# A two-model forward pass in one kernel: the prologue's token transfers, splits, banks and first two blocks rearranged

## What is computed

```python
meta = jnp.broadcast_to(meta_tokens.astype(x.dtype)[None], (b, N_META, D_MODEL))
h = jnp.concatenate([meta, x], axis=1)
...
hn = rms_norm(h, g_mix[layer])          # mean of squares, rsqrt, gain
z = h @ w_in                            # in attention_mixer, h is hn there
c_q, c_kv, k_pe, fq, fk, fv, f_logit = jnp.split(z, _offsets(ATTN_SPLITS), axis=-1)
...
bias = rel_table[t5_causal_bucket(jnp.maximum(dist, 0))]   # second model
```

## Time and profile before

| | |
|---|---|
| median of 3 runs | 1233.04 us |
| lowest, highest | 1232.21 us, 1683.81 us |
| profiled execution, its time | 1232.03 us |
| profiled execution, its span | 1230.2 us |
| PE busy | 1206.8 us, 98% of the span |
| DVE, ACT, POOL busy | 902.2, 713.7, 247.4 us |
| HBM traffic | 170 GB/s mean |

### The profile page before, as it was taken

The page is one execution under the profiler, slowest core; times in us unless marked ns, Lnnn a source line. Parts: engine busy times, 40 slices in busy tenths (PEclk is TensorE's granted clock), DMA queues, the critical chain, the costliest instruction groups (busy, mean ns, idle before and its releaser), DMA issues.

```text
span 1230.2 us, 23640 instructions
## 1 busy us (share of the span) xinstructions
PE 1206.8 (98%) x8096; PEld 1101.8 (90%) x8096; DVE 902.2 (73%) x1562; ACT 713.7 (58%) x1303; POOL 247.4 (20%) x260
## 2 busy tenths in 40 slices
PE   7999999999999999999999999999999999999997
PEld 5998899999999988888889988888889999888886
DVE  5788876555556988776568869776667988877764
ACT  4657756564444556664446876665444797666343
POOL 3000014220000114440011003442001811444000
PEclk9999999999999999999999999999999999999999
DMA  7514326555657565655556426665655644656550
GB/s 225 160 35 134 104 72 204 185 190 167 193 188 223 177 191 181 198 177 185 192 179 197 145 96 206 178 198 176 201 163 175 211 138 142 218 181 194 177 200 35
DMA packets 194922, 208.79 MB, mean 170 GB/s; under 512 B 6159, under 2 KB 183565, under 8 KB 194717
## 3 DMA queue, kind: packets, MB, share of 16 engines
q1 hardware_dynamic: 191861, 202.73, 51.7%
q10 hardware_dynamic: 2984, 5.06, 1.3%
HBM read 206.69 MB, written 2.64 MB: 170 GB/s over the span
## 4 chain that ended last, share of the span: by engine, by line
PE 86%; DVE 8%; ACT 3%; issue 2%; DMA 1%; POOL 0%; ACTq 0%; DVEq 0%; SPq 0%; POOLq 0%
PE PS L1922 27%; PE PS L1923 14%; PE PS L1916 10%; PE PS L1917 10%; PE PS L1918 9%; PE PS L2499 2%; PE PS L2500 2%; PE PS L2501 2%; DVE wlo L1075 2%; ACT whi L535 1%; PE PS L2101 1%; PE PS L2167 1%; PE PS L2145 1%; DVE x L1052 1%; PE PS L2263 1%
## 5 line engine op out<-in xcount | busy, mean ns | idle before, releaser
L535 ACT ACTIVATE whi<-raw 128x1024 fp32r<-128x1024 f32 x370 | 388.7, 1053 | 318.1 <-PE PS L1923 172.5
L1075 DVE TENSOR_TENSOR wlo<-raw,whi 128x1024 fp32r<-128x1024 f32 x370 | 454.2, 1234 | 161.4 <-ACT whi L535 158.2
L1922 PE MATMUL PS<-x,whi 128*128 128x512 f32 x832 | 291.7, 395 | 1.0 <-DVE x L1052 1.0
L1916 PE MATMUL PS<-x,whi 128*128 128x258 f32 (+2 forms) x800 | 231.9, 290 | 2.6 <-DVE wlo L1075 2.0
L1923 PE MATMUL PS<-x,wlo 128*128 128x256 f32 x832 | 234.4, 282 | 0.0
L1917 PE MATMUL PS<-x,whi 128*128 128x258 f32 (+2 forms) x800 | 228.7, 286 | 0.0
L1918 PE MATMUL PS<-x,wlo 128*128 128x258 f32 (+2 forms) x800 | 227.0, 284 | 0.0
L1922 PEld LDWEIGHTS PS<-x,whi 128*128 128x128 f32 x832 | 156.3, 188 | 37.2 <-DVE x L1052 1.6
L1825 POOL TENSOR_TENSOR act_s<-act_r 128x256 f32<-128x256 f32 (+1 forms) x128 | 142.9, 1116 | 213.4 <-ACT act_r L597 151.6
L1922 PE MATMUL PS<-hid,whi 128*128 128x512 f32 x512 | 179.0, 396 | 0.2
L1805 POOL TENSOR_TENSOR acc<-acc,sq 128x256 f32<-128x256 f32 (+2 forms) x64 | 51.8, 809 | 594.7 <-ACT sq L579 253.6
(11 more groups left out here) (323 smaller groups left out, 2009.6 us busy)
## 6 DMA issues: line engine op xcount, KB each, us to landing
raw<-in_mlp_w SPq DMA_DIRECT2D x64, 1024.0 KB, 5.3
raw<-in_w_mlp_up SPq DMA_DIRECT2D x32, 1024.0 KB, 5.5
raw<-in_w_mlp_down SPq DMA_DIRECT2D x32, 1024.0 KB, 5.0
raw<-in_w_in_conv SPq DMA_DIRECT2D x12, 1024.0 KB, 5.1
raw<-in_attn_w_in SPq DMA_DIRECT2D x12, 1024.0 KB, 5.1
raw<-in_mlstm_w_in SPq DMA_DIRECT2D x12, 1024.0 KB, 5.5
raw<-in_w_in_attn SPq DMA_DIRECT2D x9, 1024.0 KB, 5.9
raw<-in_w_out_attn SPq DMA_DIRECT2D x4, 1024.0 KB, 5.3
```

What stands on the lines that cost most here:

```text
L535: A(part_view(whi, b), raw_view(b), ACT.Copy).then_inc(w_hi, 1)
L1075: V.tensor_tensor(part_view(wlo, b), raw_view(b), f32(part_view(whi, b)), ALU.subtract).then_inc(w_lo, 1)
L1916: mm(dst, whi_b, xs_hi, start=first, stop=False)
L1922: mm(dst.rearrange("p (a t) -> p a t", a=2), std_cols(whi[b % RING], k), xs_both, start=first, stop=False)
```

## The change

Token transfer: `x_tok` comes in two transfers, features 0 to 511 (semaphore `x_in`) and 512 to 1023 (`x_right`). Meta tokens and both vector tables are issued by ACT, between the identity and the one-hot table. PE first runs 24 matmuls (`WARM`) of 256 columns on a buffer of ones (the still unused `wlo[3]`) into bank 7; their result is not read. The one-hot product moves from ahead of the token transposes to behind block 2. Transposed pieces go to eight different banks (`x_bank`), `xh` and `xl` are made straight from PSUM, and `h` is copied later; the squares read `h`. Blocks 0 and 1 are computed in halves: pieces 0 to 3 of both, then 4 to 7 of both. Blocks 4 and 5 go to banks 6 and 7, and their weights are split before the norm. The norm's matmul moves behind block 3. DVE and POOL no longer wait for `rel_out`; the bias rows lie in `act_r`, so two squares later in the layer wait for it on ACT.

```diff
-            sp.dma_start(x_tok[:, :, :], d["x"][0].rearrange("(a p) n -> p a n", p=P)).then_inc(Z["x_in"], 16)
-            sp.dma_start(meta_tok[:, :], d["meta_tokens"]).then_inc(Z["x_in"], 16)
-            sp.dma_start(vrow_a[:, :], d["v_rows_a"]).then_inc(Z["vec_in"], 16)
-            sp.dma_start(vrow_b[:, :], d["v_rows_b"]).then_inc(Z["vec_in"], 16)
+            sp.dma_start(x_tok[:, :, 0:HALF], x_rows[:, :, 0:HALF]).then_inc(Z["x_in"], 16)
+            sp.dma_start(x_tok[:, :, HALF:D], x_rows[:, :, HALF:D]).then_inc(Z["x_right"], 16)
...
             act.dma_start(ident[:, :], d["c_ident"]).then_inc(Z["const_in"], 16)
+            act.dma_start(vrow_a[:, :], d["v_rows_a"]).then_inc(Z["vec_in"], 16)
+            act.dma_start(meta_tok[:, :], d["meta_tokens"]).then_inc(Z["x_in"], 16)
+            act.dma_start(vrow_b[:, :], d["v_rows_b"]).then_inc(Z["vec_in"], 16)
...
+            def x_high(k):
+                act.wait_ge(Z["pro_t"], N_PRO + k + 1)
+                A(at(xh, k, FULL), PS[:, x_bank(k), 0:T], ACT.Copy, scale=gain(0, k)).then_inc(Z["x_hi"], 1)
...
+            def x_low(k):
+                dve.wait_ge(Z["x_hi"], k + 1)
+                stt(at(xl, k, FULL), PS[:, x_bank(k), 0:T], gain(0, k), f32(at(xh, k, FULL)), ALU.mult, ALU.subtract)\
+                    .then_inc(Z["x_ready"], 1)
...
-            dve.wait_ge(Z["rel_out"], 16)
...
+            pe.wait_ge(Z["const_set"], 5)
+            for _ in range(WARM):
+                mm(PS[:, 7, 0:2 * P], wlo[RING - 1][:, 0:P], wlo[RING - 1][:, 0:2 * P], start=True, stop=True)
             pe.wait_ge(Z["const_in"], 16)
-            pe.wait_ge(Z["const_set"], 4)
             pe.wait_ge(Z["vec_in"], 32)
             nc.tensor.transpose(PS[:, 0, 0:na], vrow_a[:, :], ident[0:na, 0:na]).then_inc(Z["pro_t"], 1)
...
+                if k == KB // 2:
+                    pe.wait_ge(Z["x_right"], 16)
...
             def a_free(o):
+                if o < 6:
+                    pe.wait_ge(Z["pro_ev"], N_PRO + (1, 2, 3, 8, 6, 7)[o])
+                    return
...
-                if j == 1:
+                if j == 2:
+                    pe.wait_ge(Z["pro_ev"], N_PRO + 5)
+                    pe.wait_ge(Z["rel_in"], 32)
+                    mm(PS[0:HEADS, 5, 0:3 * P], rel[:, :], onehot[:, :], start=True, stop=True).then_inc(Z["rel_mm"], 1)
+                if j == 3:
                     norm(0, T)
```

More of the change, by code:

```diff
@@ L643, in _, with x_square @@
                 act.dma_start(lam_in[:, n, :], bass.AP(d[name].tensor, 0, [[0, P], [1, DV]])).then_inc(Z["lam_in_s"], 16)
[L645 to L649, removed]
+            def x_high(k):
+                act.wait_ge(Z["pro_t"], N_PRO + k + 1)
+                A(at(xh, k, FULL), PS[:, x_bank(k), 0:T], ACT.Copy, scale=gain(0, k)).then_inc(Z["x_hi"], 1)
+            def x_square(k):
+                act.wait_ge(Z["pro_ev"], N_PRO + k + 1)
+                if k > 1:
+                    act.wait_ge(Z["acc_ready"], k)
+                A(sq[:, k % 2, 0:T], at(h, k, FULL), ACT.Square).then_inc(Z["sq_ready"], 1)
+            act.wait_ge(Z["pro_ev"], 1)
+            for k in range(KB // 2):
+                x_high(k)
+            split_hi(0)
+            split_hi(1)
+            for k in range(KB // 2, KB):
+                x_high(k)
+            split_hi(2)
+            for k in range(KB // 2):
+                x_square(k)
+            split_hi(3)
+            for k in range(KB // 2, KB):
+                x_square(k)
+            for b in (4, 5):
                 split_hi(b)
@@ L653, in _ @@
             A(lam[:, 2:4], lam[:, 0:2], ACT.Exp).then_inc(Z["lam_exp"], 1)
-            act.dma_start(rel_dram, rel_rows[:, :]).then_inc(Z["rel_out"], 16)
+            act.wait_ge(Z["rel_read"], 1)
+            act.dma_start(rel_dram, rel_rows).then_inc(Z["rel_out"], 16)
             act.wait_ge(Z["pro_t"], N_PRO + KB)
@@ L747, in _ @@
                         A(at(ch, c, FULL), a_z(z_in(j))[:, 0:T], ACT.Copy, scale=g).then_inc(Z["c_hi"], 1)
+                        act.wait_ge(Z["rel_out"], 16)
                         A(LATENT_SQ[c], a_z(z_in(j))[:, 0:T], ACT.Square).then_inc(Z["c_sq"], 1)
@@ L1215, in _ @@
[L1215 to L1226, removed]
@@ L1227, in _, with x_copy @@
-            low_part(0, KB - 1, FULL)
-            for b in range(1, RING):
+            def x_low(k):
+                dve.wait_ge(Z["x_hi"], k + 1)
+                stt(at(xl, k, FULL), PS[:, x_bank(k), 0:T], gain(0, k), f32(at(xh, k, FULL)), ALU.mult, ALU.subtract)\
+                    .then_inc(Z["x_ready"], 1)
+            def x_copy(k):
+                dve.wait_ge(Z["x_hi"], k + 1)
+                V.tensor_copy(at(h, k, FULL), PS[:, x_bank(k), 0:T]).then_inc(Z["pro_ev"], 1)
+            dve.wait_ge(Z["pro_t"], 2)
@@ new lines, in _ @@
+            V.tensor_copy(vec_a[:, :], PS[:, 0, 0:na]).then_inc(Z["pro_ev"], 1)
+            V.tensor_copy(vec_b[:, :], PS[:, 0, P:P + nb]).then_inc(Z["pro_ev"], 1)
+            dve.wait_ge(Z["pro_ev"], 1)
+            for k in range(KB // 2):
+                x_low(k)
+            x_copy(0)
+            split_lo(0)
+            x_copy(1)
+            split_lo(1)
+            for k in range(KB // 2, KB):
+                x_low(k)
+            x_copy(2)
+            split_lo(2)
+            for k in range(3, KB):
+                x_copy(k)
@@ L1229, in _ @@
+            for b in (3, 4, 5):
                 split_lo(b)
+            dve.wait_ge(Z["rel_mm"], 1)
+            V.tensor_scalar(rel_rows, PS[0:HEADS, 5, 0:3 * P], float(DV) ** 0.5, None, ALU.mult).then_inc(Z["rel_read"], 1)
             dve.wait_ge(Z["lam_in_s"], 64)
@@ L1832, in _ @@
             pool.wait_ge(Z["acc_ready"], 9)
+            pool.wait_ge(Z["rel_mm"], 1)
             Gp.memset(aq[FOX:FOX + 2, :, :], 1.0).then_inc(Z["pool_set"], 1)
-            pool.wait_ge(Z["rel_out"], 16)
+            pool.wait_ge(Z["lam_dot"], 2)
             pool.wait_ge(Z["pool_set"], 1)
@@ L2180, in a_join @@
                 last.then_inc(Z["a_ot"], 1)
-            for j in range(A_LEAD):
+            for j in range(2):
+                a_free(j)
+            for some in (range(KB // 2), range(KB // 2, KB)):
+                for j in range(2):
+                    if some[0] == 0:
+                        pe.wait_ge(w_lo, B["a_in"] + j + 1)
+                    for k in some:
+                        if j == 0:
+                            pe.wait_ge(Z["x_ready"], k + 1)
+                        last = product(B["a_in"] + j, k, std_cols, at(xh, k, FULL), at(xl, k, FULL), PS[:, a_bank(j), 0:T],
+                                       k == 0, k == KB - 1)
+                    if some[-1] == KB - 1:
+                        last.then_inc(w_used, 1)
+            for j in range(2, A_LEAD):
                 if j == A_LEAD - 1:
```

35 lines of the change are left out of this document (20 added, 15 removed).

## The result

The changed kernel took 1234.37 us (median of 20 runs, 1232.66 to 1236.69) against 1233.05 us of the kernel before (20 runs on the same chip). The ratio is 1.0015, with a 95% interval of 1.0008 to 1.0022. So it is slower, by 1.3 us, where 1.2 us faster was forecast. The difference is small, well within 2%, but the interval leaves out 1. The profiled execution took 1233.44 us, the second fastest of the 20, with a span of 1231.6 us, 1.4 us above the 1230.2 us of before.

What follows compares the result with a forecast made beforehand. PE was taken as the bound, a matmul in flight 98% of the span. Block 6 moving from 37.89 to 36.7 us gains 1.2: profiled 1232.03 to 1230.8, median 1231.8 us; range 1228.3 to 1235.0 us.

Steps and rivals of the forecast that it cites:

- When block 0 can start: Start of PE's weight matmuls: weights, their splits and a bank copy let block 0 start at 14.8 us, before 16.02.
- one of the two signs of being wrong: Token transposes: forecast wrong if the first piece comes after 9 us; the other sign is a later shift that isn't constant.
- the rival on late tables: Vector tables in ACT's queue land late; kernel loses if after 8.8 us; at 10 us, 1234.2 us; chance 0.12.
- Clock: PE's clock at block 0: half speed again despite the ones, for 2.4 us, losing 1.1 us.
- Clock held: Rival: block 0 runs at full speed, block 6 at 35.8 us, gain 2.1 us, 1230.9 us; chance 0.2.
- From block 0 to the norm: Four blocks, one-hot product and clock loss put the norm's matmul at 28.8 us, 3.7 us later than before.
- From the norm to block 6: Chain through ACT and DVE takes 7.9 us; PE waits 1.3 us; block 6 at 36.7 us, 1.2 us gained.
- Blocks 7 and later have slack: After block 6: each low part is one DVE step of 1.26 us plus a read-out, against 3.5 us of PE.
- have several microseconds: Forget-gate rows, the next thing with a fixed delay after block 6: claimed slack of several microseconds.
- everything after it shifted by one constant: Sign: block 6 starts near 36.7 us and all later work moves by one constant; otherwise the forecast is wrong.
- The slower rival: Same as the rival on late tables: vector tables at 10 us would give 1234.2 us; chance 0.12.

Runs made afterwards that it cites:

- run 2: Changed kernel with the norm's matmul moved into the middle of block 3, on PE alone: 1233.9 us, ratio 1.0009.
- run 8: run 5 with 40 matmuls on ones instead of 24: 1231.33 us, ratio 0.9988.
- run 1: Changed kernel with ACT's two forget-gate steps moved behind `head_rstd(0)`: 1232.93 us, ratio 1.0000.
- run 9: Changed kernel with only the edit of run 6 (32 ones, two 240-column matmuls on ones ahead of each piece): 1233.78 us, ratio 1.0008.
- run 6: run 5 with 32 ones and two 240-column matmuls on ones ahead of each transposed piece: 1230.38 us, ratio 0.9982.
- run 10: Kernel before, with only 24 matmuls on ones added ahead of its transposes: 1232.96 us, ratio 0.9998.
- run 7: run 5 with meta tokens and vector tables issued by SP between the token halves: 1232.40 us, ratio 0.9999.
- run 3: run 2 plus ACT's `norm(0, FULL)` ahead of the lambda exponential and four transfers, against the changed kernel: 1232.52 us, ratio 0.9995.
- run 4: Changed kernel without the matmuls on ones (`WARM` from 24 to 0): 1234.88 us, ratio 1.0019.
- run 5: Changed kernel with the edits of run 1 and run 3 together: 1231.06 us, ratio 0.9991.

## Why the prediction was wrong

**When block 0 can start: right.** 14.8 us was forecast and 14.81 us measured, with group 0's high part at 12.04 us (12.0). Pieces took 0.53 us at full clock instead of 0.42, and the first began at 9.09 us instead of 8.5, since the tables' own transposes started at 8.83 us; the wait for the weights hid both. This lies past one of the two signs of being wrong, a first piece after 9 us, and at the edge of the rival on late tables (tables after 8.8 us, pieces after 9.3), but block 0 was not late, so that rival is not the cause.

**Clock: right in kind, short in size.** It was low again when block 0 started, and that cost 3.3 us at half pace instead of 2.4: 0.9 / 0.227 x 0.1 = 0.4 us more. What I had not seen is that the fall can come in the middle of the transposes, 4.0 us after the ones. The rule of the Trainium skill quoted with the rival "Clock held" (TensorE: Matmul & The Clock Gate, Part 1, recent activity) would give this rival only if transposes count as activity; here, and in run 2 (10.0 us, in the second piece), the clock fell while PE was busy with transposes. But in both PE had stood still between the ones and the tables (1.55 and 1.86 us), and in run 8, without such a pause, the clock stayed up through 4.5 us of transposes and 1.4 us of waiting. What transposes do for the clock is therefore open.

**From block 0 to the norm: right**, 29.35 us for 28.8, of which 0.4 us is the clock.

**From the norm to block 6: right as a mechanism, a little short.** The wait for the low part is there, 1.10 us for 1.3; ready +8.2 us after the norm for +7.9, because ACT's transfers were not done early: they stand behind the exponential of the lambda products, which DVE computed only at 28.25 to 28.60 us, behind the low part of block 5 and the read-out of the one-hot product (27.78 us). They ended at 30.25 us, and the logarithm came at +0.95 us, near its old +1.1 and not at the +0.65 us that early transfers would have given. Block 6 came at 37.55 instead of 36.7 us: gain 0.34 for 1.2.

**The step that failed** is the last of the prediction's part on the norm and block 6, "Blocks 7 and later have slack", with its sentence on the forget-gate rows, "have several microseconds", and with them "everything after it shifted by one constant". I had followed only the low parts on DVE and looked at the forget gate for its own consumer, the rows sent later. But its exponential stands in ACT's order ahead of `head_rstd(0)`, and so behind it waits a head sum of PE. The slack was in the trace of before: `ars` at 39.64 us against the sum at 41.09 us. In the changed kernel the sum starts 0.61 us after `ars` starts; 39.64 + 0.61 = 40.25 us, so before there was 0.84 us of slack (the sum came at 41.09 us), not several. The row arrives 2.34 us later, and PE 0.30 us earlier (40.79 us without the wait): 2.34 - 0.84 + 0.30 = 1.80 us, the wait measured. This only splits up one set of times; the test is run 1, which takes the wait away alone. The slower rival had the right sign and the wrong mechanism. The range held the time because of that rival's bound, and so by luck.

**What stays open:** the changed kernel spreads over 4.0 us where the one before stays within 1.4, leaving out its one run at 1683.81. A part of it goes with the clock: the five longest of the 20 executions (1236.41 to 1236.69 us) have the lowest mean granted clock, 0.993, where the others have 0.994 to 0.997. Run 9, with the clock held, still spreads over 2.7 us, and run 6 over 1.2, so the clock isn't all of it. I have no profile of one of the long executions of the changed kernel.

Another part arises far behind the start. The same weight split on DVE starts at 989.00 us before, 990.38 us in the changed kernel and 990.09 us in run 10. Measured at several such splits, run 10 is within 0.1 us of the kernel before at 682 us, 0.36 us behind at 873 us, and 1.09 us behind at 989 us. The profiles of runs 2, 7, 8, 9 and 10 all fall back by 0.7 to 1.4 us between 873 and 989 us, under a granted clock of 1.00 and where no edit reaches; that of the changed kernel and those of runs 1, 3, 4, 5 and 6 do not. Run 5 gains 0.7 us between 563 and 682 us in the same way. The cause is open. It means that the last matmul of one profile can be off by more than the effects sought here, while the waits in the first 50 us tell what an edit did.

## What to carry to other kernels

A step that is moved later must be followed through every engine that works in order, to each wait behind it and not just to the next: here norm, DVE row, forget gate, `head_rstd(0)`, head sum. Read the slack of each such wait from the trace before (when the releaser was done, when the waiter came), and put steps whose input comes late, and an engine's transfer issues, behind what the bounding engine needs next. An earlier start or a held clock that only lets the bounding engine arrive sooner at such a wait gives little: the head sum came 0.28 us earlier in run 9, and 4.0 us earlier with the row out of the way as well in run 6.

## What the runs showed of the hardware

- The granted clock fell during the transposes of 128 x 128 or the pause ahead of them, and not at one moment: 4.0 us after the last matmul on ones in the changed kernel (7.3 to 11.3 us), 3.2 us in runs 1 and 7, 3.0 us in run 2 (7.0 to 10.0), 2.8 us in run 10, 2.6 us in run 5 (6.7 to 9.3) and 2.1 us in run 3 (6.4 to 8.5, PE still idle). The shorter the 24 ones had taken, that is, the earlier they had got the full clock, the earlier it fell: they took 5.49, 5.45 and 5.46, 5.23, 5.13, 4.90 and 4.56 us in these.
- It stayed at 1.00 up to block 0 in the profiles of runs 6 and 9 (32 ones, and two 240-column matmuls ahead of each piece) and of run 8 (40 ones alone, 5.9 us from the last of them to block 0). Transposes alone did not raise it: from 8.70 us to block 0 at 15.71 us in run 4, and block 0 still began at half pace.
- The rise differs as much: from 2.5 us into block 0 in run 1 (17.3 us) and 3.3 us in the changed kernel (18.1 us) to 4.9 us in run 2 (20.2 us).
- A profile whose clock never rose before block 0, as that of the kernel before and of run 4, shows 1.00 for the granted clock in these windows, where the matmuls' spacing of 0.23 us shows half. The record is to be read with the spacing beside it.
- The queue and place in which small transfers are issued moved landings by more than a microsecond: the first transpose from 8.97 us in run 5 to 7.57 us in run 7, the high part of group 0 from 13.05 us, when ACT was free for it, to 13.73 us, when the landing released it. In the changed kernel the landing released it at 12.04 us.
- Issuing a transfer took 0.30 to 0.45 us of ACT each ahead of the norm's logarithm, and four in a row held it up: it started 1.52 us behind the norm's matmul in run 9 (28.52 to 30.04 us), 0.66 us behind it in run 3, where they stood behind it.
